# 446 columns per block for the seven-product pairs of the encoder's FFN, 398 and 382 for the plain blocks, rows at multiples of 64 bytes

## What is computed

```python
h = _rms(x, norm1_g)
proj = h @ w_in
...
attn = _window_attention(q, k, v, sink)
a, gate = jnp.split(c, 2, axis=-1)
u = a * jax.nn.sigmoid(gate)
u = _dwconv(u, conv_dw_w, conv_dw_b)
u = jax.nn.silu(_layernorm(u, conv_ln_g, conv_ln_b))
x = x + jnp.concatenate([attn, u], axis=-1) @ w_out
h2 = _rms(x, norm2_g)
g = jax.nn.silu(_dwconv(h2 @ ffn_w_gate, ffn_dw_w, ffn_dw_b))
x = x + (g * (h2 @ ffn_w_up)) @ ffn_w_down
```

## Time and profile before

| | us |
|---|---|
| median of 3 runs | 2601.6 (2598.65 to 2601.61) |
| the profiled execution, its own time | 2601.34 |
| its span, first to last instruction | 2599.6 |
| TensorE (PE) busy | 2578.2, 99% |
| VectorE (DVE) busy | 1863.2, 72% |
| ScalarE (ACT) busy | 1267.9, 49% |
| A and first O slots (to 520) | 520 |
| G, D and O slots (520 to 1488.7) | 968.7 |
| pairs (1488.7 to the end) | 1110.9 |

### The profile page before, as it was taken

One profiled execution on the slowest core, in us unless ns is written; L12 is line 12 of the kernel. 1 busy time (PEld: TensorE's weight loads), 2 busy tenths in 40 slices (PEclk: granted clock), 3 DMA queues, 4 the chain that ended last, 5 costly groups with the idle time before them and its releaser, 6 DMA issues. The chain is left out here.

```text
span 2599.6 us, 35531 instructions
## 1 busy us (share of the span) xinstructions
PE 2578.2 (99%) x12927; PEld 2292.5 (88%) x12927; DVE 1863.2 (72%) x3099; ACT 1267.9 (49%) x2179; POOL 184.4 (7%) x316
## 2 busy tenths in 40 slices
PE   8999999999999999999999999999999999999999
PEld 6877777788878888888788899999999999999999
DVE  4765658887887698877883686757658875765765
ACT  6345554468347835683572444425335443433532
POOL 0110021101011111010101100000000100000000
PEclk9999999999999999999999999999999999999999
DMA  9967779734554475447439531212213521122212
GB/s 351 342 229 232 260 283 335 276 120 163 209 198 144 144 288 183 155 155 267 146 123 357 185 129 62 67 60 66 65 59 121 167 65 60 62 65 62 66 57 69
DMA packets 139757, 419.15 MB, mean 161 GB/s; under 512 B 24160, under 2 KB 38880, under 8 KB 122944
## 3 DMA queue, kind: packets, MB, share of 16 engines
q1 hardware_dynamic: 113632, 317.98, 36.2%
q0 software_dynamic: 25952, 98.91, 10.4%
HBM read 328.03 MB, written 88.79 MB: 160 GB/s over the span
## 5 line engine op out<-in xcount | busy, mean ns | idle before, releaser
L1463 ACT ACTIVATE part_hi<-part_raw 128x512 fp32r<-128x512 f32 x396 | 247.9, 628 | 406.5 <-DMA part_raw<-w_pass_t 161.7
L2207 PE MATMUL bank<-hw_hi,weights 128*128 128x452 f32 (+1 forms) x1408 | 420.1, 373 | 0.0
L1737 DVE SCALAR_TENSOR_TENSOR cc<-win,par,cc 128x512 f32<-128x512 f32 x600 | 408.1, 742 | 0.0
L2367 PE MATMUL bank<-mid,part_hi 128*128 128x416 f32 x1408 | 380.9, 351 | 2.0 <-DVE mid L1972 1.7
L1916 DVE TENSOR_TENSOR part_lo<-part_raw,part_hi 128x512 fp32r<-128x512 f32 x396 | 270.5, 687 | 141.8 <-ACT part_hi L1463 135.6
L2159 PE MATMUL bank<-h_hi,weights 128*128 128x512 f32 x1104 | 357.5, 397 | 0.0
L2207 PEld LDWEIGHTS bank<-hw_hi,weights 128*128 128x128 f32 x1408 | 264.9, 188 | 36.2 <-issue 12.3
L2367 PEld LDWEIGHTS bank<-mid,part_hi 128*128 128x128 f32 x1408 | 263.9, 188 | 6.3 <-DVE mid L1972 3.1
L2207 PE MATMUL bank<-hw_lo,weights 128*128 128x450 f32 (+1 forms) x704 | 258.8, 368 | 0.0
L2159 PEld LDWEIGHTS bank<-h_hi,weights 128*128 128x128 f32 x1104 | 207.2, 188 | 56.2 <-issue 5.1
L1986 DVE TENSOR_TENSOR pair_y<-bank,pair_y 128x416 f32<-128x416 f32 x192 | 112.1, 589 | 190.5 <-PE bank L2367 190.4
(11 more groups left out here) (220 smaller groups left out, 4301.8 us busy)
## 6 DMA issues: line engine op xcount, KB each, us to landing
weights<-weight_scratch SPq DMA_DIRECT2D x88, 1024.0 KB, 6.2
wraw<-w_ffn_t SPq DMA_DIRECT2D x88, 512.0 KB, 3.5
part_raw<-w_ffn_t SPq DMA_DIRECT2D x176, 256.0 KB, 2.7
weight_scratch<-weights POOLq DMA_DIRECT2D x22, 1024.0 KB, 7.7
wraw<-w_down_t SPq DMA_DIRECT2D x44, 512.0 KB, 3.6
part_raw<-w_pass_t SPq DMA_DIRECT2D x88, 256.0 KB, 2.6
cat_hi<-cat_scratch SPq DMA_DIRECT2D x10, 1024.0 KB, 6.9
cat_lo<-cat_scratch SPq DMA_DIRECT2D x10, 1024.0 KB, 9.1
```

Of the source, the lines that this page charges most:

```text
L1463: nc.scalar.activation(p_hi[k % HI_RING][:], p_raw[part_of(k)][:], ACT.Copy).then_inc(s_whi, 1)
L1737: nc.vector.scalar_tensor_tensor(acc, win[i][:, tap:tap + TB], w_tap, acc, ALU.mult, ALU.add).then_inc(s_cv, 1)
L2207: mm = nc.tensor.matmul(out, l[:, k, :], r[:, k, 1:TC + 1] if s else r[:, k, :], start=(k == 0 and j == 0), stop=(k == KT - 1 and j == 2))
L2367: mm = nc.tensor.matmul(bank[BANK_Y[n % 4]][:, 0:TP], l[:, (deep * o + t) % KH, :], mid2[:, t, part, i, :], start=(t == 0 and z == 0), sto ...
```

## The change

The pairs take 446 columns in place of 416, and the two plain windows 398 and 382 in place of 450 and 450; the total stays 2564. A row of a tile that a matmul reads gets a pitch of a multiple of 16 columns (64 bytes), and only its first columns are used. Region starts and sizes are rounded to 256 bytes or follow new maxima: `R_Y` is now 36864 bytes behind `R_MID`. Two of the four `v` buffers move. The descriptor space of GpSimd's DMAs is 4096 bytes per partition in place of the default 16384.

```diff
-TP = 416
-TC = 2 * -(-(TOKENS + 1 - 2 * PAIRS * TP) // (2 * PLAIN))
-OUT_COLS = TC * PLAIN + 2 * TP * PAIRS
+TP = 446
+WIDTH = (398, 382)
+TC = max(WIDTH)
+OUT_COLS = sum(WIDTH) + 2 * TP * PAIRS
...
+def pitch(cols):
+    return -(-cols // 16) * 16
...
-    return TC * min(w, PLAIN) + TP * max(w - PLAIN, 0)
+    return sum(WIDTH[:w]) + TP * max(w - PLAIN, 0)
...
-        R_Y = R_MID + up(4 * FH * 2 * TC)
-        R_SM = R_Y + up(4 * KT * TC)
-        R_HW = R_SM + 2 * up(4 * TH) + 2 * up(4 * TC)
-        R_SIDE = R_HW + 2 * up(4 * KT * TH)
+        def up256(n):
+            return -(-n // 256) * 256
+
+        B_PITCH, P_PITCH = pitch(TQ), pitch(TP)
+        B_BYTES, E_BYTES, V_BYTES, W_BYTES, Y_BYTES = 4 * KH * B_PITCH, up256(4 * TQ), up256(4 * TP), 4 * KH * P, up256(4 * KT * TP)
+        M_BYTES = 4 * 4 * 2 * 2 * P_PITCH
+        M_PITCH, H_PITCH = pitch(TC), pitch(TH)
+        R_Y = R_MID + max(up(4 * FH * 2 * M_PITCH), H + 2 * 4 * TB + H)
+        R_SM = max(R_Y + up256(4 * KT * TC), R_D + 4 * B_BYTES + 3 * E_BYTES + M_BYTES + 2 * Y_BYTES + V_BYTES)
+        R_HW = R_SM + up256(2 * up(4 * TH) + 2 * up(4 * TC))
+        R_SIDE = max(R_HW + 2 * up(4 * KT * H_PITCH), R_SM + (HI_RING + 5) * W_BYTES + 2 * V_BYTES + H)
...
-        mid, = run(R_MID, ("mid", [P, FH, 2, TC], F32R))
+        mid = run(R_MID, ("mid", [P, FH, 2, M_PITCH], F32R))[0][:, :, :, 0:TC]
...
-        hw_hi, = run(R_HW, ("hw_hi", [P, KT, TH], F32R))
+        hw_hi = run(R_HW, ("hw_hi", [P, KT, H_PITCH], F32R))[0][:, :, 0:TH]
...
-            b_hi[b], = run(hi_at[b], (f"{b}_hi", [P, KH, TQ], F32R))
+            b_hi[b] = run(hi_at[b], (f"{b}_hi", [P, KH, B_PITCH], F32R))[0][:, :, 0:TQ]
...
-        mid2, = run(m_at, ("mid2", [P, 4, 2, 2, TP], F32R))
+        mid2 = run(m_at, ("mid2", [P, 4, 2, 2, P_PITCH], F32R))[0][:, :, :, :, 0:TP]
...
-                out = bank[out_bank(e)][:, 0:TC if s else TH]
+                cols = slice(1, WIDTH[w] + 1) if s else slice(0, WIDTH[w] + 2)
+                out = bank[out_bank(e)][:, 0:cols.stop - cols.start]
...
-    nc = bacc.Bacc("TRN2", target_bir_lowering=False, num_devices=1)
+    nc = bacc.Bacc("TRN2", target_bir_lowering=False, num_devices=1, dynamic_dma_scratch_size=4096)
```

More of the change, by code:

```diff
@@ L45 @@
 PLAIN, PAIRS = 2, 2
-TP = 416
-TC = 2 * -(-(TOKENS + 1 - 2 * PAIRS * TP) // (2 * PLAIN))
-OUT_COLS = TC * PLAIN + 2 * TP * PAIRS
+TP = 446
+WIDTH = (398, 382)
+TC = max(WIDTH)
+OUT_COLS = sum(WIDTH) + 2 * TP * PAIRS
+assert len(WIDTH) == PLAIN and OUT_COLS > TOKENS
 PAD_COLS = OUT_COLS + 2
@@ L598, in encoder_layer @@
         cv = run(R_SM + 2 * up(4 * TH), ("cv0", [P, TC], F32), ("cv1", [P, TC], F32))
[L599 to L601 removed]
+        hw_hi = run(R_HW, ("hw_hi", [P, KT, H_PITCH], F32R))[0][:, :, 0:TH]
+        hw_lo = run(R_HW + up(4 * KT * H_PITCH), ("hw_lo", [P, KT, H_PITCH], F32R))[0][:, :, 0:TH]
+        hw_raw = run(R_HW + up(4 * KT * H_PITCH), ("hw_raw", [P, KT, H_PITCH], F32))[0][:, :, 0:TH]
         h_hi1, h_lo1 = run(R_D, ("h_hi1", [P, KT, TB], F32R), ("h_lo1", [P, KT, TB], F32R))
@@ L831, in x2_stores @@
             return 16 * KT * (c + 1)
-        X_FROM = (R_X - R_MID) // (2 * 4 * TC)
+        X_FROM = (R_X - R_MID) // (2 * 4 * M_PITCH)
         @block.sync
@@ L1415, in window_high @@
                 act.wait_ge(s_hw[p], 16 * (w + 1))
-                nc.scalar.activation(hw_hi[:, PK * p:PK * (p + 1), :], hw_raw[:, PK * p:PK * (p + 1), :], ACT.Copy) \
-                  .then_inc(s_hwhi, 1)
+                part = (slice(None), slice(PK * p, PK * (p + 1)), slice(0, WIDTH[w] + 2))
+                nc.scalar.activation(hw_hi[part], hw_raw[part], ACT.Copy).then_inc(s_hwhi, 1)
             def gate_copy(w, h, i):
@@ L1851, in window_low @@
                 dve.wait_ge(s_hwhi, PIECES * w + p + 1)
-                part = slice(PK * p, PK * (p + 1))
-                nc.vector.tensor_tensor(hw_lo[:, part, :], hw_raw[:, part, :], hw_hi[:, part, :].bitcast(F32),
-                                        ALU.subtract).then_inc(s_hwlo, 1)
+                part = (slice(None), slice(PK * p, PK * (p + 1)), slice(0, WIDTH[w] + 2))
+                nc.vector.tensor_tensor(hw_lo[part], hw_raw[part], hw_hi[part].bitcast(F32), ALU.subtract).then_inc(s_hwlo, 1)
             def gate_conv(w, h, i):
@@ L1889, in y_add @@
                     dve.wait_ge(s_y, d_index(w, 0, o) + 1)
-                nc.vector.tensor_tensor(yb[:, o, :], bank[out_bank(OUTPUT["D", w, h, o])][:, 0:TC], yb[:, o, :],
-                                        ALU.add).then_inc(s_y, 1)
+                t = yb[:, o, 0:WIDTH[w]]
+                nc.vector.tensor_tensor(t, bank[out_bank(OUTPUT["D", w, h, o])][:, 0:WIDTH[w]], t, ALU.add).then_inc(s_y, 1)
             def part_sum(gi, a):
@@ L2203, in gate_up @@
                 a, b = whi[n % RING], wlo[n % RING]
-                out = bank[out_bank(e)][:, 0:TC if s else TH]
+                cols = slice(1, WIDTH[w] + 1) if s else slice(0, WIDTH[w] + 2)
+                out = bank[out_bank(e)][:, 0:cols.stop - cols.start]
                 for k in range(KT):
                     for j, (l, r) in enumerate(((a, hw_hi), (a, hw_lo), (b, hw_hi))):
-                        mm = nc.tensor.matmul(out, l[:, k, :], r[:, k, 1:TC + 1] if s else r[:, k, :],
+                        mm = nc.tensor.matmul(out, l[:, k, :], r[:, k, cols],
                                               start=(k == 0 and j == 0), stop=(k == KT - 1 and j == 2))
@@ L2222, in down @@
                     for j, (l, part) in enumerate(((a, 0), (a, 1), (b, 0))):
-                        mm = nc.tensor.matmul(out, l[:, q, :], mid[:, k, part, :],
+                        mm = nc.tensor.matmul(out, l[:, q, :], mid[:, k, part, 0:WIDTH[w]],
                                               start=(k == 0 and j == 0), stop=(k == FH - 1 and j == 2))
```

42 lines of the change are left out of this document (21 added, 21 removed).

## The result

The changed kernel takes 2613.09 us, the median of 4 runs (2610.85 to 2614.55), against 2600.96 for the kernel before, run beside it: a ratio of 1.0046, interval [1.0033, 1.0059]. It is slower by 12 us, where 32 us less were forecast. The profiled execution took 2614.13 us for a span of 2612.3, 12.8 us more than the one before.

A forecast was written before the change was run, and what follows sets the result against it. TensorE, 99% busy, was taken as the bound, through its matmuls' start-to-start distances. 54.6 - 87.9 - 7.6 + 4 + 4 = -32.9 us on 2601.34 gave 2569 us, range 2553 to 2600, chance 0.78.

The forecast's parts named there:

- The waits, 4 + 4 us in the forecast: TensorE waits: +4 us in the plain stretch (0 to 12), +4 at the last LayerNorm's `cat_lo` (0 to 8).
- the 7.6 forecast: Chunks 0, 2 and 4: 984 matmuls fall from 234.4 to 226.7 ns with `h_hi0` aligned, -7.6 us.
- feels only lateness beyond: Plain stretch: tiles are split two slots ahead, some 9 us, so TensorE notices only greater lateness; +4 us.
- The pairs, +54.6 us in the forecast: Pairs: 446 columns for 416 take matmuls from 190.7 to 200.1 ns, times 5808: +54.6 us (+51 to +73).
- The remainder of 14 ns: Pairs: time per matmul above its columns' 186.1 ns, taken near chunk 3's; bounds 13.4 and 17.1.
- The correlation in the earlier trace: Matmul remainder smallest where every row starts at a multiple of 256 bytes, 3 to 8 ns more where rows start anywhere.
- The plain windows, -87.9 us: Plain windows: matmuls of 182.1 and 175.4 ns against 206.5, 1584 in each window: -87.9 us (-96 to -79).
- The last `cat_lo` wait: Last LayerNorm: shorter slots ahead of `cat_lo` make TensorE wait +4 us more, bounds 0 and 8.
- Columns alone: Rival, all matmuls: remainder the same whatever the address, A slots give nothing, waits add 8; 2603 us, chance 0.09.
- The weight load is a floor: Rival, plain windows: the weight load sets the pace, so matmuls stop at 190.7 ns; about 2606 us, chance 0.04.
- VectorE and ScalarE bound the plain stretch: Rival, plain stretch: VectorE's 165.6 us idle is latency that doesn't shrink; 2630 us, from 41 us of waits, chance 0.09.

The follow-up runs named there:

- thinned pair: Convolution taps after the first on 128 of 512 columns, in the changed kernel (2597.34 us, 0.9978) and in the kernel before (2598.43 us, 0.9987).
- LayerNorm forms: Changed kernel with LayerNorm steps of chunks 2 and 3 later (2619.48 us), spaced differently (2617.19), or statistics matmuls reading `ones` (2617.09).
- first LayerNorm form: Changed kernel with the LayerNorm steps of chunks 2 and 3 later by a slot or more: 2619.48 us, ratio 1.0066.
- kernel with the wider pitch: Changed kernel with 464 in place of 448 columns from row to row of the pairs' windows: 2611.66 us, one execution.
- second LayerNorm form: Changed kernel with another spacing of the LayerNorm steps of chunks 2 and 3: 2617.19 us, ratio 1.0065.
- kernel without the rounding: Changed kernel without the rounding of a row to 16 columns: 2617.95 us, one execution.
- thinned kernel: Changed kernel with every convolution tap but the first on 128 of its 512 columns: 2597.34 us, ratio 0.9978.
- half move: Changed kernel with 430 columns for the pairs and 422 and 420 for the plain windows: 2600.35 us, ratio 0.9991.

## Why the prediction was wrong

The forecast said -32.9 us, the profiled execution shows +12.8. The 45.7 us between them come from three of its steps: 23 from the waits with the clock, 14 from the pairs, 8 from the plain windows. Of its bounds only that of the waits was broken; the pairs and the plain windows stayed inside theirs. All of its bounds together reach to +13 us, and +12.8 lies just inside that reach, outside the range of 2553 to 2600 us that was forecast.

**The waits, 4 + 4 us in the forecast, 12 + 8 at most: 31 us.** Before the first G phase 6.7 us of the 7.6 forecast went to stops of 2.8 us for the norm of q and k at 374 and 3.7 for `cat_lo` at 407, and to the 6.8 us at half the clock behind it; in the plain stretch 24.4 us stand where 8 were put. The step that failed is the sentence that TensorE "feels only lateness beyond" the two slots by which a tile is split ahead, and its bound of 12. It priced the weight tiles and the chain of the gate, and those are not what TensorE waits for: the list names LayerNorm sums, maxima, normalising and copies of scores, which share the same queues of VectorE and ScalarE and have no two slots of lead. VectorE's idle time is 130.8 us (819.6 less 688.8) in the stretch, more than the forecast's 96 for want of the expected shrink, and still not enough where it matters: 80% busy over the third G phase, it had nothing free just ahead of the stop at 1038.7. The thinned pair shows that VectorE's time is on the changed kernel's path, the LayerNorm forms that moving these steps doesn't mend it. That the squares wait for ScalarE's order is read from one place of one timeline.

**A cost that the forecast did not have: the clock.** It is a part of those 31 us. Some 11 us went to 23.8 us at 1.2 GHz behind stops of TensorE. The profile of the kernel before showed no such stretch, and the forecast took its clock as given.

**The pairs, +54.6 us in the forecast: +68.7.** The remainder of 14 ns, taken from chunk 3, was too small; 202.5 ns is 16.4 above the 186.1 of the columns. Gates alone, on rows of 1792 bytes as the argument wanted them, have 206.5 less 186.7, 19.8 ns: 1848 of them at 5.8 ns over their forecast are 11 of the 14 us. The correlation in the earlier trace rows holds for `h_hi0`, as its shift shows, and was carried over to rows where it doesn't hold. The rows are also one slot each: over whole chunks the kernel before has 233.9 ns in chunk 2 and 228.4 in chunk 3, a difference of 5.5 and not 7.7, and a remainder of 15.1 in chunk 3, not 13.4.

**The plain windows, -87.9 us: -79.5.** The same step. 16 ns was taken; 185.2 and 177.2 ns less the 166.1 and 159.4 of the columns leave 18 to 19. The 209.6 ns of D slots in the earlier trace rows are of one slot too; their mean is 206.0, which hardly moves the 206.5 that the forecast starts from.

**What held.** The distance is columns at 2.4 GHz and a remainder; down to 175 ns there is no floor from the weight load, though LDWEIGHTS still shows 190 ns in the groups of the changed kernel. Chunks 0, 2 and 4 fall to 227 to 228 ns, by their means a gain of 6 us. The descriptor space costs nothing. The last `cat_lo` wait grew by 3.3 us, to 4.2, where 4 were forecast.

```profile
L2222 PEld LDWEIGHTS bank<-hw_hi,weights 128*128 128x128 f32 x1407 | 261.5, 190 | 13.2 <-issue 12.6
```

**The rivals.** "Columns alone" was right for the windows: 30 columns at 5808 matmuls are 72.6 us (+68.7 came) and 60 at 3168 are 79.2 (79.5 came). It was wrong on chunks 0, 2 and 4 and on the waits. The Trainium skill (TensorE: Matmul & The Clock Gate, Back-to-back issue gap) gives N/2.4 and a fixed gap of 2.5 ns, as the isolated distance of one matmul. Its slope is what the runs show on average; above it stand 13 to 21 ns here, in streams with a weight load for each matmul. "The weight load is a floor" falls. "VectorE and ScalarE bound the plain stretch" is the mechanism that decided, at 0.09 in the forecast, with a wrong price: it took all of their idle time for latency, and its 41 us of waits were never reached. What came is between the two: 24 us of waits in the stretch and 8 of clock, and with distances that by themselves bring 18 us this, and the 7 us ahead of it, are enough to turn the sign.

**What stays open.** Why a row's start moves the distance of a matmul by some ns, and why for gates in one layout and for up products in another. Which stop is followed by half the clock: of those between 2.5 and 3.4 us some were and some were not, even in the same place. The stop of 2.7 us near 912 was followed by it in the first LayerNorm form and in the kernel with the wider pitch, and the one as long at 914 in the changed kernel was not; the longest ones without such a stretch are of 3.7 us, at 1288 in the second LayerNorm form, and of 3.8, at 1070 in the kernel without the rounding. Executions of one kernel differ in it too, as those of the thinned one do: the kernel before has mean clocks of 0.998 to 1.000, and its longest time, 2608.57 us, at 0.998. And how the waits that remain in the thinned kernel divide between ScalarE's order and the length of the chain; an order with the squares ahead of the weight tile was not tried.

## What to carry to other kernels

Moving matmul columns out of a stretch in which two other engines are 75 to 80% busy is worth only what these can follow; the bound to work out is not their idle time in the stretch but what they have to finish just ahead of each matmul that waits for them, and every kind of such a matmul has to be priced, not only the one that the change touches. A stop of TensorE costs its length and may cost a stretch at half the clock behind it, so a change that trades work for waits should be charged for both, and moving half as much may be free where moving all isn't. An address effect seen in one pair of stretches should be tried there alone before it is built into a layout: here one shift by 64 bytes gave 6 us, and the new pitches at the old widths gave none, since what the A slots gained the D slots and the pairs lost.

## What the runs showed that was not expected

- A stop of TensorE of 3.7 to 4.6 us inside a stream that is otherwise full was followed by 3.4 or 6.8 us with a granted clock of 0.50 in the changed kernel, every time; in the other kernels this holds for all stops of that length or longer but two, of 3.7 and 3.8 us. Stops of 2.5 to 3.4 us were followed by it in some places and not in others. Each such stretch costs 1.5 to 3 us, on top of the stop.
- The start of a row in memory changes the distance of matmuls on 512 columns: means of 234 ns where `h_hi0` starts 192 bytes past a multiple of 256, 229 at 128 past (the old widths and the half move, both with the new layout), 227 to 228 at the multiple. On 448 columns gates went from 206.5 to 202.1 ns with another pitch; on 450 columns the new layout left G slots as they were and made D slots 2.6 ns slower.
- Taking TensorE's waits for the sums away did not shorten the kernel at all (ratio 1.0062 against 1.0046): it came to other waits, for maxima, `attn_lo` and the copies of transposed scores, each of 3.5 us or more at the longest.
